# Second feed-forward: convolution with tokens on the partitions, gates shifted by DMA, only the gated units turned

## Chip, cores and metric

The kernel runs on one core of one Trainium2 chip. The metric is the device time of one execution in microseconds. A profiled execution is one execution with the hardware profiler on; its span runs from the first to the last instruction.

## What is computed

Two transformer blocks on one sequence of 256 tokens of width 2048, in float32. The first has attention, gated linear attention and a short convolution, and a feed-forward; the second has windowed attention, a state space model, and a feed-forward with a convolution. Only the last matters here:

```python
val, gate = jnp.split(h @ w_up[i], 2, axis=-1)    # h: 256 tokens x 2048, normed; val ("up") and gate: 5632 columns
gate = causal_depthwise_conv(gate, conv_w[i], conv_b[i])
x = x + (val * jax.nn.gelu(gate, approximate=False)) @ w_down[i]

def causal_depthwise_conv(x, w, b):               # along the tokens
    xp = jnp.pad(x, ((0, 0), (CONV_WIDTH_2 - 1, 0), (0, 0)))
    y = b
    for k in range(CONV_WIDTH_2):                 # CONV_WIDTH_2 = 3
        y = y + w[k] * xp[:, k:k + l]
    return y
```

## The kernel before

**Panels and pieces.** Each large product is cut into panels of 512 output columns. A panel of the feed-forward has 2048 rows of weights, 4 chunks of 512 rows; a chunk (1 MB) is one load into one of 4 slots, and is used as two pieces of 256 rows. Float32 accuracy is had by splitting both operands into a high and a low part (float32r), with three matmuls for each product: high by high, low by high, high by low. A piece is 12 matmuls of 512 columns: 2 blocks of 128 rows, 2 halves of 128 tokens, 3 matmuls. The stationary side is the activation, turned so that features lie on the partitions (xT_hi, xT_lo, hiddenT_hi, hiddenT_lo); results come out with tokens on the partitions (panels, in PSUM, two banks for each of two panels at a time).

**Who does what.** The five engines' programs are written out by hand, each in a class of its own, tied by semaphores. SyncE issues the weight loads (L370), each when the low half of the last piece of the chunk four earlier is done. ScalarE writes the high half of piece g+3 (`split`, L1225) when TensorE has finished piece g-1 (a ring of 4 pieces). VectorE writes the low half behind it (L1803). TensorE waits for `lo_split` before each piece. After each piece every engine may take one step of side work (`side.step()`): generators whose `yield`s say in which step each part is issued. On VectorE and ScalarE the step comes right behind the half of piece g+3.

**The feed-forwards.** `ffn` runs over 11 pairs of panels, gate and then up. ScalarE evacuates the gate panel into `FF1` (L1377), VectorE the up panel into `FF2`. In the first feed-forward the gate is passed through Silu, VectorE multiplies at the evacuation (L1966), and TensorE turns the product, 8 transposes of 128x128 (`tr`, L619) in one side step of the next pair's gate panel; ScalarE and VectorE write hiddenT_hi and hiddenT_lo from PSUM. In the second (`second` is true) gate and up are evacuated as they are (L1963) and both turned, 16 transposes; with features on the partitions the convolution is a multiplication by a scalar for each partition and tap, with the tokens shifted along the row: `conv2` (L2001, L2007), Gelu (L1396), the product with the turned up (`gate2`, L2019), high (L1398) and low part (L2023). The weights of the convolution lie in `V2`, one column for each block of 128 features. They are loaded in the opening as rows of 128 elements (`vectors`, L1302: seven small loads; `load_rows4`, L1283 to L1286: five more) and turned by TensorE (`turn_rows`).

**Queues.** Loads issued by ScalarE stand in its own instruction stream (shown as ACTq) and share the 16 DMA engines with SyncE's weight loads. Each adds 16 to a semaphore when it has landed.

Of the kernel before, what the change touches and what calls it, by code (L numbers as in the profile page):

```python
# [14 lines left out]
P = 128  # L15
# [75 lines left out]
class Events:  # L91
# [8 lines left out]
        mixed ffn_turned hidden_hi hidden_lo convolved gelu_ready gated_ready rows_applied  # L100
# [8 lines left out]
    LOADS = """x_load0 x_load1 x_load2 x_load3 x_load4 second_piece fourth_piece rows0 rows1 rows2 rows3 rows4 decay gla_b norm_rows dt b_proj c_proj v_bias sinks  # L109
        gate_rows0 gate_rows1 glu_rows stores""".split()  # L110
# [11 lines left out]
class Memory:  # L122
# [10 lines left out]
    def on_chip(self):  # L133
# [20 lines left out]
        self.V2 = small("vectors2", [P, 4 * KF])  # L154
# [55 lines left out]
        self.CG = sb("conv_gelu", [P, 2, S], R + 96 * K)  # L210
# [55 lines left out]
        self.ROWS = [sb(f"rows{i}", [P, P], 90 * K + R + 512 * i) for i in range(5)]  # L266
# [226 lines left out]
class Tensor:  # L493
# [8 lines left out]
    def program(self):  # L502
# [44 lines left out]
        self.ffn(plan.ffn1, side, False)  # L547
# [29 lines left out]
        self.ffn(plan.ffn2, side, True)  # L577
# [123 lines left out]
    def ffn(self, panels, side, second):  # L701
        m = self.m
        X = (m.XH, m.XL)
        for i, (gate, up) in enumerate(panels):
            if i:
                side.add(self.ffn_turn(panels[i - 1], second, spread=True))
            self.panel(gate, X, side)
            self.panel(up, X, side)
            side.finish()
        side.add(self.ffn_turn(panels[-1], second, spread=False))  # L710

    def ffn_turn(self, pair, second, spread):
# [3 lines left out]
        for kp in range(2):  # L716
            for pan in pair:
                for t in range(TT):
                    pe.wait_ge(*pan.evac[t])
            self.ffn_turns += 1  # L720
            n = self.ffn_turns
            if second:
                b0, b1 = self.bank(2 * kp), self.bank(2 * kp + 1)
                for k in range(2):
                    for t in range(TT):
                        f = (2 * kp + k) * P
                        o = slice(k * S + t * P, k * S + (t + 1) * P)
                        self.tr(b0[:, o], m.FF1[:, t, f:f + P])
                        inst = self.tr(b1[:, o], m.FF2[:, t, f:f + P])
                self.free(2 * kp, "gated_ready", n - 2 * (FF // PANEL))  # L730
                self.free(2 * kp + 1, "gated_ready", n - 2 * (FF // PANEL))
            else:
                inst = self.four(self.bank(kp), lambda k, t: m.FF2[:, t, k * P:(k + 1) * P], 2 * kp)
                self.free(kp, "hidden_lo", n)
            inst.then_inc(ev["ffn_turned"])
        for _ in range((5 if second else 4) if spread else (4 if second else 2)):
            yield
        if not spread:
            for _ in range(5 if second else 0):
                yield  # L740
# [375 lines left out]
class Scalar:  # L1116
# [161 lines left out]
    def load_rows4(self):  # L1278
        act, t, rows, ev = self.act, self.t, self.m.ROWS[4], self.ev
        vec = lambda x: x.rearrange("(k p) -> k p", p=P)  # L1280
        at = 0
        for n in ("norm2_w", "attn_norm_g_2", "ffn_norm_g_2"):
            act.dma_start(rows[at:at + KD, :], vec(t[n][0])).then_inc(ev["loaded_rows4"], 16)  # L1283
            at += KD
        act.dma_start(rows[at:at + 2, :], vec(t["gla_norm_w"][0])).then_inc(ev["loaded_rows4"], 16)
        act.dma_start(rows[at + 2:at + 26, :],  # L1286
                      t["conv_w"][0].rearrange("j (k p) -> (j k) p", p=P)).then_inc(ev["loaded_rows4"], 16)
# [6 lines left out]
    def vectors(self):  # L1294
        act, t, m, ev = self.act, self.t, self.m, self.ev
        vec = lambda x: x.rearrange("(k p) -> k p", p=P)
        cw = t["conv_w_2"][0].rearrange("j (k p) -> (j k) p", p=P)
        for i, at, n, src in ((1, 0, 88, cw[0:88, :]), (2, 0, 44, cw[88:132, :]), (2, 44, 44, vec(t["conv_b_2"][0])),
                              (3, 0, 14, vec(t["b_in_2"][0, 0:QKVU2])), (3, 14, 4, vec(t["ssm_d_2"][0])),
                              (3, 18, ST, t["ssm_a_re_2"][0].rearrange("(s q) p -> s (q p)", q=2)),  # L1300
                              (3, 34, ST, t["ssm_a_im_2"][0].rearrange("(s q) p -> s (q p)", q=2))):
            act.dma_start(m.ROWS[i][at:at + n, :], src).then_inc(ev[f"loaded_rows{i}"], 16)  # L1302
        self.load_rows4()
        for _ in range(7):
            yield
        for i, dst, n in ((1, m.V2[:, 0:88], 88), (2, m.V2[:, 88:176], 88), (3, m.V3[:, 0:50], 50),
                          (4, m.V1[:, KD:90], 74)):
# [56 lines left out]
    def ffn(self, panels, side, second, rows):  # L1364
        act, m, ev = self.act, self.m, self.ev
        n0 = 2 * len(panels) if second else 0
        for i, (gate, up) in enumerate(panels):
            if i:
                side.add(self.ffn_turn(i - 1, second, spread=True))
            self.panel(gate, side)  # L1370
            act.wait_ge(ev["multiplied"], gate.end)
            if i and second:
                act.wait_ge(ev["ffn_turned"], n0 + 2 * i)
            for t in range(TT):
                if i:
                    act.wait_ge(*panels[i - 1][1].evac[t])
                act.activation(m.FF1[:, t, :], m.ACC[:, (gate.index % 2) * TT + t, :],  # L1377
                               ACT.Copy if second else ACT.Silu, scale=m.RSTD[:, t:t + 1]).then_inc(gate.evac[t][0])
            self.panel(up, side)
            side.finish()  # L1380
        side.add(self.ffn_turn(len(panels) - 1, second, spread=False, rows=rows, pair=panels[-1]))

    def ffn_turn(self, i, second, spread, rows=None, pair=None):
# [4 lines left out]
        for kp in range(2):  # L1388
# [3 lines left out]
            if second:  # L1392
                yield
                k = n - 2 * (FF // PANEL)
                act.wait_ge(ev["convolved"], k)
                act.activation(m.CG[:, :, :], m.CG[:, :, :], ACT.Gelu).then_inc(ev["gelu_ready"])  # L1396
                act.wait_ge(ev["gated_ready"], k)
                act.activation(hh, m.CG[:, :, :], ACT.Copy).then_inc(ev["hidden_hi"])  # L1398
            else:
                act.wait_ge(ev["ffn_turned"], n)  # L1400
                act.activation(hh, m.SIDE[:, kp, :], ACT.Copy).then_inc(ev["hidden_hi"])
            yield
            if spread and kp == 0:
                yield
                if not second:
                    yield
# [287 lines left out]
class Vector:  # L1694
# [162 lines left out]
    def vectors(self):  # L1857
        for _ in range(7):
            yield
        for i in (1, 2, 3, 4):  # L1860
# [87 lines left out]
    def ffn(self, panels, side, second):  # L1948
        dve, m, ev = self.dve, self.m, self.ev
        n0 = 2 * len(panels) if second else 0  # L1950
        for i, (gate, up) in enumerate(panels):
            if i:
                side.add(self.ffn_turn(i - 1, second, spread=True))
            self.panel(gate, side)
            self.panel(up, side)
# [12 lines left out]
        side.add(self.ffn_turn(len(panels) - 1, second, spread=False))  # L1968

    def ffn_turn(self, i, second, spread):  # L1970
# [4 lines left out]
        for kp in range(2):  # L1975
            self.ffn_turns += 1
            if second:
                self.conv2(at, kp)
                yield
                self.gate2(at, kp)  # L1980
            else:
                k = slice(at + 2 * kp, at + 2 * kp + 2)
# [490 lines left out]
```

## Time and profile before

| | |
|---|---|
| median of 3 runs | 2894.95 us (2894.95 to 2894.97) |
| profiled execution | 2894.78 us, of which span 2893.5 us |
| TensorE busy | 2879.7 us, 13528 matmuls and transposes |
| VectorE, ScalarE busy | 1632.5 us, 1321.2 us |
| DMA | 536.86 MB, 186 GB/s in the mean |
| TensorE's granted clock, mean | 0.999 |

Busy times are those of one profiled execution. Matmuls overlap in the profile (each is shown longer than the distance to the next), so distances between starts say more than durations. A releaser behind an arrow is the instruction whose end let the waiting one start. PE is TensorE, ACT ScalarE, DVE VectorE, SP SyncE; ACTq and SPq are the DMA instructions on those engines' streams.

### The profile page before, as it was taken

The page shows a single profiled execution, that of the slowest core. Times are in us where ns is not written, and L with a number is a line of the kernel's source. Part 1 is how long each engine was busy: PE and PEld are TensorE (multiplying, and loading weights), DVE is VectorE, ACT ScalarE, POOL GpSimd, SP SyncE. Part 2 cuts the span into 40 slices and gives each one's busy share as a digit, 9 for nine tenths or more (in the row PEclk, how much of TensorE's full clock was granted, in tenths as well). Part 3 has the DMA queues.
Part 4 walks back from the last instruction along what each step waited for, and adds up shares of the span by engine and source line. Part 5 has one row for each costly group of instructions (what it writes and reads, how often), then busy time and mean ns, then how long its engine had stood idle before and what let it go on. Part 6 is the DMA issues. An engine that isn't in the chain of part 4 may idle for free.

```text
span 2893.5 us, 32574 instructions
## 1 busy us (share of the span) xinstructions
PE 2879.7 (100%) x13528; PEld 2379.0 (82%) x13528; DVE 1632.5 (56%) x1874; ACT 1321.2 (46%) x1627; POOL 182.2 (6%) x221
## 2 busy tenths in 40 slices
PE   9999999999999999999999999999999999999998
PEld 8878887788888888888888888887888888888887
DVE  5464555555555554554474457655755665656444
ACT  5444445444444444444454455444554444444443
POOL 0000000000000000000000029900100000000000
PEclk9999999999999999999999999999999999999999
DMA  7655454555555556555665555554655555555563
GB/s 252 197 167 194 155 192 148 174 189 189 193 188 187 189 189 190 189 190 189 205 193 183 185 175 198 171 171 153 205 188 189 188 178 189 183 193 191 187 204 131
DMA packets 279392, 536.86 MB, mean 186 GB/s; under 512 B 17361, under 2 KB 20365, under 8 KB 279245
## 3 DMA queue, kind: packets, MB, share of 16 engines
q1 hardware_dynamic: 267520, 528.52, 56.0%
q10 hardware_dynamic: 11725, 6.27, 0.8%
q8 instruction: 107, 1.75, 0.2%
q14 instruction: 40, 0.33, 0.0%
HBM read 532.65 MB, written 2.10 MB: 185 GB/s over the span
## 4 chain that ended last, share of the span: by engine, by line
PE 99%; DVE 1%; ACT 0%; issue 0%; POOL 0%; POOLq 0%; ACTq 0%; DVEq 0%
PE panels L595 32%; PE panels L597 31%; PE panels L596 31%; PE side L619 3%; DVE weights_lo L1803 0%; PE side L911 0%; PE side L608 0%; PE side L988 0%; PE side L907 0%; PE side L896 0%; PE side L775 0%; PE side L1080 0%; PE side L1081 0%; PE side L1057 0%; PE side L792 0%; PE side L809 0%
## 5 line engine op out<-in xcount | busy, mean ns | idle before, releaser
L1803 DVE TENSOR_TENSOR weights_lo<-weights,weights_hi 128x1024 fp32r<-128x1024 f32 (+1 forms) x1032 | 1252.9, 1219 | 1080.6 <-ACT weights_hi L1225 1078.0
L1225 ACT ACTIVATE weights_hi<-weights 128x1024 fp32r<-128x1024 f32 (+1 forms) x1032 | 1066.4, 1036 | 1220.2 <-PE panels L597 1205.9
L595 PE MATMUL panels<-weights_hi,xT_hi 128*128 128x512 f32 (+1 forms) x2752 | 1078.2, 392 | 0.2
L597 PE MATMUL panels<-weights_hi,xT_lo 128*128 128x512 f32 (+1 forms) x2752 | 1068.4, 388 | 0.0
L596 PE MATMUL panels<-weights_lo,xT_hi 128*128 128x512 f32 (+1 forms) x2752 | 1067.8, 388 | 0.0
L595 PEld LDWEIGHTS panels<-weights_hi,xT_hi 128*128 128x128 f32 x2752 | 516.8, 188 | 112.1 <-issue 7.3
L597 PEld LDWEIGHTS panels<-weights_hi,xT_lo 128*128 128x128 f32 x2752 | 516.6, 188 | 107.9
L596 PEld LDWEIGHTS panels<-weights_lo,xT_hi 128*128 128x128 f32 x2752 | 517.0, 188 | 103.2 <-issue 0.2
L595 PE MATMUL panels<-weights_hi,hiddenT_hi 128*128 128x512 f32 x704 | 274.9, 391 | 0.0
L597 PE MATMUL panels<-weights_hi,hiddenT_lo 128*128 128x512 f32 x704 | 274.0, 389 | 0.0
L596 PE MATMUL panels<-weights_lo,hiddenT_hi 128*128 128x512 f32 x704 | 273.9, 389 | 0.0
L597 PEld LDWEIGHTS panels<-weights_hi,hiddenT_lo 128*128 128x128 f32 x704 | 132.1, 188 | 27.4
L596 PEld LDWEIGHTS panels<-weights_lo,hiddenT_hi 128*128 128x128 f32 x704 | 132.2, 188 | 27.2
L595 PEld LDWEIGHTS panels<-weights_hi,hiddenT_hi 128*128 128x128 f32 x704 | 132.2, 188 | 27.2
L402 POOL TENSOR_TENSOR rstd<-mean_squares,minus_half 128x2 f32<-128x2 f32 x5 | 3.5, 697 | 1270.6 <-DVE mean_squares L1866 1270.6
L595 PE MATMUL panels<-weights_hi,merged2T_hi 128*128 128x512 f32 x128 | 50.4, 393 | 0.3 <-issue 0.3
L595 PE MATMUL panels<-weights_hi,mixedT_hi 128*128 128x512 f32 x128 | 50.2, 392 | 0.0
L597 PE MATMUL panels<-weights_hi,merged2T_lo 128*128 128x512 f32 x128 | 49.9, 390 | 0.0
L597 PE MATMUL panels<-weights_hi,mixedT_lo 128*128 128x512 f32 x128 | 49.9, 390 | 0.0
L596 PE MATMUL panels<-weights_lo,merged2T_hi 128*128 128x512 f32 x128 | 49.8, 389 | 0.0
L596 PE MATMUL panels<-weights_lo,mixedT_hi 128*128 128x512 f32 x128 | 49.8, 389 | 0.0
L402 POOL TENSOR_TENSOR rstd_first<-mean_squares,minus_half 128x2 f32<-128x2 f32 x1 | 0.7, 691 | 737.9 <-DVE mean_squares L1866 737.9
(354 smaller groups left out, 1912.7 us busy)
## 6 DMA issues: line engine op xcount, KB each, us to landing
weights<-in_w_in SPq DMA_DIRECT2D x162, 1024.0 KB, 5.0
weights<-in_w_up SPq DMA_DIRECT2D x88, 1024.0 KB, 5.1
weights<-in_w_ffn_gate SPq DMA_DIRECT2D x44, 1024.0 KB, 5.1
weights<-in_w_ffn_up SPq DMA_DIRECT2D x44, 1024.0 KB, 5.2
weights<-in_w_out SPq DMA_DIRECT2D x32, 1024.0 KB, 5.2
weights<-in_w_ffn_down SPq DMA_DIRECT2D x32, 1024.0 KB, 5.1
weights<-in_w_down SPq DMA_DIRECT2D x32, 1024.0 KB, 5.1
weights<-in_w_ffn_down SPq DMA_DIRECT2D x16, 768.0 KB, 4.5
```

The source lines that it names most:

```text
L402: self.pool.tensor_tensor(dst[:, 0:2], self.m.MS[:, 0:2], self.m.NHALF[:, 0:2], ALU.pow).then_inc(self.ev["rstd_ready"])
L595: pe.matmul(acc, a, wh, start=k0 + k == 0, stop=False)
L596: pe.matmul(acc, a, wl, start=False, stop=False)
L597: inst = pe.matmul(acc, b, wh, start=False, stop=k0 + k == total - 1)
L619: return self.pe.transpose(out, in_, self.m.IDENT[0:in_.shape[0], 0:in_.shape[0]])
L1225: self.act.activation(self.m.HI[:, g % PIECES, 0:n], raw, ACT.Copy).then_inc(self.ev["hi_split"])
L1803: self.dve.tensor_tensor(m.LO[:, ring, 0:n], raw, m.HI[:, ring, 0:n].bitcast(F32), ALU.subtract).then_inc(self.ev["lo_split"])
```

## The change

In the second feed-forward the convolution is done with tokens on the partitions, before anything is turned. ScalarE evacuates the gate panel into `FF1` as before and then issues, for each pair, four copies from SBUF to SBUF: the gates shifted by one token (`GS1`) and by two (`GS2`), each as one copy within partitions 0 to 127-s and one that carries the last tokens of the first half over to the first partitions of the second. The weights of the three taps and the bias are loaded from HBM for each pair as rows of 512 columns, broadcast to all 128 partitions (`WR1`, `WR2`, four loads, a panel ahead). VectorE does the convolution in six operations over both token halves at once (`conv2`), spread over the side steps of the up panel; ScalarE does one Gelu; VectorE multiplies at the evacuation of the up panel, as in the first feed-forward, and TensorE turns the product alone with the same code as there. `V2`, its three small loads and its two turns in the opening are gone. Shapes: `FF1`, `GS1`, `GS2` are [128, 2, 512] in float32.

The diff, cut to what the prediction speaks of:

```diff
+        self.GS1 = sb("gate_shifted1", [P, TT, PANEL], R + 96 * K)
+        self.GS2 = sb("gate_shifted2", [P, TT, PANEL], 80 * K + 512)
+        self.WR1 = sb("conv_rows01", [P, 2, PANEL], R + 40 * K)
+        self.WR2 = sb("conv_rows2b", [P, 2, PANEL], R + 84 * K)
...
-        for i, n, loads in ((1, 88, 1), (2, 88, 2), (3, 50, 4), (4, 74, 5)):
+        for i, n, loads in ((1, 50, 4), (2, 74, 5)):
...
-            if second:
-                b0, b1 = self.bank(2 * kp), self.bank(2 * kp + 1)
-                for k in range(2):
-                    for t in range(TT):
-                        f = (2 * kp + k) * P
-                        o = slice(k * S + t * P, k * S + (t + 1) * P)
-                        self.tr(b0[:, o], m.FF1[:, t, f:f + P])
-                        inst = self.tr(b1[:, o], m.FF2[:, t, f:f + P])
-                self.free(2 * kp, "gated_ready", n - 2 * (FF // PANEL))
-                self.free(2 * kp + 1, "gated_ready", n - 2 * (FF // PANEL))
-            else:
-                inst = self.four(self.bank(kp), lambda k, t: m.FF2[:, t, k * P:(k + 1) * P], 2 * kp)
-                self.free(kp, "hidden_lo", n)
-            inst.then_inc(ev["ffn_turned"])
-        for _ in range((5 if second else 4) if spread else (4 if second else 2)):
+            self.four(self.bank(kp), lambda k, t: m.FF2[:, t, k * P:(k + 1) * P], 2 * kp).then_inc(ev["ffn_turned"])
+            self.free(kp, "hidden_lo", n)
+        for _ in range(4 if spread else 2):
             yield
         if not spread:
-            for _ in range(5 if second else 0):
-                yield
...
+        if second:
+            side.add(self.conv_rows(panels[0][0], self.plan.out2[-1].end))
...
             self.panel(gate, side)
             act.wait_ge(ev["multiplied"], gate.end)
-            if i and second:
-                act.wait_ge(ev["ffn_turned"], n0 + 2 * i)
             for t in range(TT):
                 if i:
                     act.wait_ge(*panels[i - 1][1].evac[t])
                 act.activation(m.FF1[:, t, :], m.ACC[:, (gate.index % 2) * TT + t, :],
                                ACT.Copy if second else ACT.Silu, scale=m.RSTD[:, t:t + 1]).then_inc(gate.evac[t][0])
+            if second:
+                side.finish()
+                self.shift_gates(gate)
+                side.add(self.gelu(i, panels))
             self.panel(up, side)
...
+    def conv_rows(self, gate, end):
+        act, m, ev, t = self.act, self.m, self.ev, self.t
+        act.wait_ge(ev["multiplied"], end)
+        cols = slice(gate.col - FF, gate.col - FF + PANEL)
+        for dst, src in ((m.WR1[:, 0, :], t["conv_w_2"][0][0, cols]), (m.WR1[:, 1, :], t["conv_w_2"][0][1, cols]),
+                         (m.WR2[:, 0, :], t["conv_w_2"][0][2, cols]), (m.WR2[:, 1, :], t["conv_b_2"][0][cols])):
+            act.dma_start(dst, src.partition_broadcast(P)).then_inc(ev["loaded_conv_rows"], 16)
+        yield
+
+    def shift_gates(self, gate):
+        act, m, ev = self.act, self.m, self.ev
+        self.wait_evacuated(gate)
+        for s, dst in ((1, m.GS1), (2, m.GS2)):
+            act.dma_start(dst[s:P, :, :], m.FF1[0:P - s, :, :]).then_inc(ev["loaded_shifted"], 16)
+            act.dma_start(dst[0:s, 1, :], m.FF1[P - s:P, 0, :]).then_inc(ev["loaded_shifted"], 16)
+
+    def gelu(self, i, panels):
+        act, m, ev = self.act, self.m, self.ev
+        for _ in range(6):
+            yield
+        act.wait_ge(ev["convolved"], i + 1)
+        act.activation(m.FF1[:, :, :], m.FF1[:, :, :], ACT.Gelu).then_inc(ev["gelu_ready"])
+        if i + 1 < len(panels):
+            yield from self.conv_rows(panels[i + 1][0], panels[i][0].end)
...
         dve, m, ev = self.dve, self.m, self.ev
         n0 = 2 * len(panels) if second else 0
+        if second:
+            dve.memset(m.GS1[0:1, 0, :], 0.0)
+            dve.memset(m.GS2[0:2, 0, :], 0.0)
         for i, (gate, up) in enumerate(panels):
             if i:
-                side.add(self.ffn_turn(i - 1, second, spread=True))
+                side.add(self.ffn_turn(i - 1, spread=True))
             self.panel(gate, side)
+            if second:
+                side.finish()
+                side.add(self.conv2(i))
             self.panel(up, side)
             side.finish()
             dve.wait_ge(ev["multiplied"], up.end)
             if i:
                 dve.wait_ge(ev["ffn_turned"], n0 + 2 * i)
             for t in range(TT):
-                acc, r = m.ACC[:, (up.index % 2) * TT + t, :], m.RSTD[:, t:t + 1]
                 if second:
-                    dve.tensor_scalar(m.FF2[:, t, :], acc, r, None, ALU.mult).then_inc(up.evac[t][0])
+                    dve.wait_ge(ev["gelu_ready"], i + 1)
                 else:
                     dve.wait_ge(*gate.evac[t])
-                    dve.scalar_tensor_tensor(out=m.FF2[:, t, :], in0=acc, scalar=r, in1=m.FF1[:, t, :],
-                                             op0=ALU.mult, op1=ALU.mult).then_inc(up.evac[t][0])
...
+    def conv2(self, i):
+        dve, m, ev, step = self.dve, self.m, self.ev, self.step
+        w0, w1, w2, bias = (r[:, j, :].unsqueeze(1).to_broadcast([P, TT, PANEL]) for r in (m.WR1, m.WR2) for j in range(2))
+        g = m.FF1[:, :, :]
+        yield
+        yield
+        dve.wait_ge(ev["loaded_shifted"], 16 * 4 * (i + 1))
+        dve.wait_ge(ev["loaded_conv_rows"], 16 * 4 * (i + 1))
+        step(dve.tensor_tensor(g, g, w2, ALU.mult))
+        for shifted, w in ((m.GS1, w1), (m.GS2, w0)):
+            yield
+            step(dve.tensor_tensor(shifted[:, :, :], shifted[:, :, :], w, ALU.mult))
+            step(dve.tensor_tensor(g, g, shifted[:, :, :], ALU.add))
+        yield
+        dve.tensor_tensor(g, g, bias, ALU.add).then_inc(ev["convolved"])
+        yield
```

## Rows read from the trace of the kernel before

**Rows 1.** Page: busy times and granted clock.

```profile
PE 2879.7 (100%) x13528; PEld 2379.0 (82%) x13528; DVE 1632.5 (56%) x1874; ACT 1321.2 (46%) x1627; POOL 182.2 (6%) x221
...
PEclk9999999999999999999999999999999999999999
```

**Rows 2.** All waits of PE.

```profile
PE side L608 <- POOL identity L408: 1.6, 1, 1.6
PE side L619 <- DMA x<-in_x: 1.0, 1, 1.0
PE panels L595 <- issue: 0.3, 1, 0.3
```

**Rows 3.** Chain of work: start us, us, what, in three stretches.

```profile
48.44 0.56 PE side L619 x4
...
1036.62 0.87 PE side L619 x8
...
1081.06 0.87 PE side L619 x8
...
2239.41 1.75 PE side L619 x16
2284.70 1.75 PE side L619 x16
```

**Rows 4.** Timeline of ACT and DVE: start us, us, engine line op [idle before <-releaser].

```profile
2228.56 1.06 ACT L1225 ACTIVATE weights_hi<-weights 128x1024 fp32r<-128x1024 f32 x1 [1.60 <-PE panels L597]
...
2229.65 1.23 DVE L1803 TENSOR_TENSOR weights_lo<-weights,weights_hi 128x1024 fp32r<-128x1024 f32 x1 [1.43 <-ACT weights_hi L1225]
...
2257.53 1.27 ACT L1377 ACTIVATE ffn_gate<-panels,rstd 128x512 f32<-128x512 f32 x2 [1.54 <-PE panels L597]
```

**Rows 5.** Tile conv_gelu: duration ns min/median/max, first and last start.

```profile
L2007 DVE SCALAR_TENSOR_TENSOR conv_gelu<-side,vectors,conv_gelu x88: 470/480/485, 2196.0 to 2655.0; 128x255 f32<-128x255 f32 x44, 128x254 f32<-128x254 f32 x44
L2001 DVE TENSOR_SCALAR conv_gelu<-side,vectors x44: 533/538/545, 2195.0 to 2653.1; 128x256 f32<-128x256 f32 x44
```

**Rows 6.** Groups by form, 128x1024 operands: count, busy us, mean ns.

```profile
L2031 DVE TENSOR_TENSOR projected_a<-projected_a 128x1024 f32<-128x1024 f32 x2 | 2.4, 1220 | 0.0
...
L1683 ACT ACTIVATE merged<-merged 128x1024 f32<-128x1024 f32 x4 | 4.2, 1049 | 0.0
```

**Rows 7.** Tile ffn_hidden, evacuation in the first feed-forward.

```profile
L1966 DVE SCALAR_TENSOR_TENSOR ffn_hidden<-panels,rstd,ffn_gate x22: 741/748/751, 986.8 to 1431.8; 128x512 f32<-128x512 f32 x22
```

**Rows 8.** DMA issues: KB each, median us to landing.

```profile
weights<-in_w_up SPq DMA_DIRECT2D x88, 1024.0 KB, 5.1
...
c_twice<-in_ssm_c_re ACTq DMA_DIRECT2D x2, 128.0 KB, 2.3
```

**Rows 9.** DMA in 2454 to 2458.2, one weight load: GB/s in 40 slices, packets.

```profile
GB/s 312 234 293 410 371 429 449 351 410 449 371 390 468 371 390 410 449 371 429 410 293 234 176 117 59 0 0 0 0 0 0 0 0 0 0 0 0 0 0 0
DMA packets 459, 0.91 MB, mean 216 GB/s; under 512 B 16, under 2 KB 16, under 8 KB 459
```

**Rows 10.** DMA queue of ACT in 34 to 46: packets, MB, share.

```profile
q10 hardware_dynamic: 445, 0.15, 4.9%
```

**Rows 11.** DMA queue of SP: whole span (page), then 2885 to 2893.5 (stores).

```profile
q1 hardware_dynamic: 267520, 528.52, 56.0%
...
q1 hardware_dynamic: 848, 2.10, 64.1%
```

**Rows 12.** Timeline, DMA issues on ACT's queue: start us, us.

```profile
1441.05 4.50 ACTq L1528 DMA_DIRECT2D b_im<-in_ssm_b_im  x1
...
1762.07 0.35 ACTq L1677 DMA_DIRECT2D gate_bias_rows<-in_b_in  x1
```

**Rows 13.** Granted clock after the last matmul (third from the right), and PE's opening.

```profile
2887.50:2889.00 1.50, 0.00 (x0) 0.00 (x0) 0.67 (x2) 0.55 (x1) 0.00 (x0) 0.52 0.95 363
...
1.59 3.78 PE L608 MATMUL side<-identity 128*128 128x128 f32 x16 [1.59 <-POOL identity L408]
...
7.27 1.50 PE L608 MATMUL side<-identity 128*128 128x128 f32 x12
```

More of the change, by code:

```diff
@@ L265, in on_chip @@
         self.FF2 = sb("ffn_hidden", [P, TT, PANEL], R + 92 * K)
-        self.ROWS = [sb(f"rows{i}", [P, P], 90 * K + R + 512 * i) for i in range(5)]
+        self.ROWS = [sb(f"rows{i}", [P, P], 90 * K + R + 512 * i) for i in range(3)]
 class Plan:
@@ L546, in program @@
         self.residual(plan.out1, (m.MH, m.ML), side, rows=False, turn=True)
-        self.ffn(plan.ffn1, side, False)
+        self.ffn(plan.ffn1, side)
         side.add(self.ssm_setup())
@@ L699, in residual, with ffn @@
             side.add(self.norm_panel(p, pan, rows, turn))
-    def ffn(self, panels, side, second):
+    def ffn(self, panels, side):
         m = self.m
@@ L705, in ffn @@
             if i:
-                side.add(self.ffn_turn(panels[i - 1], second, spread=True))
+                side.add(self.ffn_turn(panels[i - 1], spread=True))
             self.panel(gate, X, side)
@@ L709, in ffn, with ffn_turn @@
             side.finish()
-        side.add(self.ffn_turn(panels[-1], second, spread=False))
-    def ffn_turn(self, pair, second, spread):
+        side.add(self.ffn_turn(panels[-1], spread=False))
+    def ffn_turn(self, pair, spread):
         pe, ev, m = self.pe, self.ev, self.m
@@ L1378, in ffn, with ffn_turn @@
                                ACT.Copy if second else ACT.Silu, scale=m.RSTD[:, t:t + 1]).then_inc(gate.evac[t][0])
+            if second:
+                side.finish()
+                self.shift_gates(gate)
+                side.add(self.gelu(i, panels))
             self.panel(up, side)
             side.finish()
-        side.add(self.ffn_turn(len(panels) - 1, second, spread=False, rows=rows, pair=panels[-1]))
-    def ffn_turn(self, i, second, spread, rows=None, pair=None):
+        side.add(self.ffn_turn(len(panels) - 1, spread=False, rows=rows, pair=panels[-1]))
+    def conv_rows(self, gate, end):
[20 more added lines that the diff above has]
+            yield from self.conv_rows(panels[i + 1][0], panels[i][0].end)
+    def ffn_turn(self, i, spread, rows=None, pair=None):
         act, m, ev = self.act, self.m, self.ev
@@ L1391, in ffn_turn @@
             hh = m.HH[:, at + 2 * kp:at + 2 * kp + 2, :]
[L1392 to L1401, printed above, removed]
+            act.wait_ge(ev["ffn_turned"], n)
+            act.activation(hh, m.SIDE[:, kp, :], ACT.Copy).then_inc(ev["hidden_hi"])
             yield
@@ L1859, in vectors @@
             yield
-        for i in (1, 2, 3, 4):
+        for i in (1, 2):
             self.dve.wait_ge(self.ev["vectors"], i + 1)
@@ L1950, in ffn @@
         n0 = 2 * len(panels) if second else 0
+        if second:
+            dve.memset(m.GS1[0:1, 0, :], 0.0)
+            dve.memset(m.GS2[0:2, 0, :], 0.0)
         for i, (gate, up) in enumerate(panels):
             if i:
-                side.add(self.ffn_turn(i - 1, second, spread=True))
+                side.add(self.ffn_turn(i - 1, spread=True))
             self.panel(gate, side)
+            if second:
+                side.finish()
+                side.add(self.conv2(i))
             self.panel(up, side)
@@ L1976, in ffn_turn @@
             self.ffn_turns += 1
[L1977 to L1982, printed above, removed]
-                self.dve.wait_ge(self.ev["hidden_hi"], self.ffn_turns)
-                self.dve.tensor_tensor(m.HL[:, k, :], m.SIDE[:, kp, :], m.HH[:, k, :].bitcast(F32),
-                                       ALU.subtract).then_inc(self.ev["hidden_lo"])
+            k = slice(at + 2 * kp, at + 2 * kp + 2)
+            self.dve.wait_ge(self.ev["hidden_hi"], self.ffn_turns)
+            self.dve.tensor_tensor(m.HL[:, k, :], m.SIDE[:, kp, :], m.HH[:, k, :].bitcast(F32),
+                                   ALU.subtract).then_inc(self.ev["hidden_lo"])
             yield
```

79 lines of the change are left out of this document (21 added, 58 removed).

## Prediction

> **What bounds the kernel now.** First the page's busy times: TensorE is busy for all but 13.8 us of the span, VectorE for 56% and ScalarE for 46%, at a granted clock of 9 tenths or more in every slice [rows 1]. Then the waits of TensorE: three, 2.9 us together, all in the opening [rows 2]. So only two kinds of edit move the end: fewer or shorter TensorE instructions, and anything that makes TensorE wait where it does not wait today. The stage to read is the second feed-forward. The chain view shows the first feed-forward too, whose turning already has the form that the change gives the second: a turn there is 8 transposes in 0.87 us and pairs of panels follow at 1081.06 - 1036.62 = 44.44 us; in the second it is 16 transposes in 1.75 us and the step is 2284.70 - 2239.41 = 45.29 us [rows 3]. Taking the turn out, 43.57 us are left for the 16 pieces of a pair, 2.72 us each. That is the pulse to which all else is compared.
>
> **TensorE's own work.** 88 of 176 transposes of the stage go (gate and up were both turned, now the product alone): 0.88 us by the blocks, 0.85 by the steps, I take 0.87; 11 pairs give 9.6 us. Two of four turns of weight rows go from the opening, half of 0.56 us [rows 3], 0.3. These are on the path in full, since TensorE waits for nothing there. Sum: 9.9 us. The profiled execution (2894.78 us, a span of 2893.5 and 1.3 around it) stands 0.17 under the median of 2894.95, from which I count: 2885.1 if nothing else changed.
>
> **The reserve under which the rest must stay.** ScalarE's high half of piece g+3 starts when TensorE starts piece g (it waits for TensorE each time) and takes 1.06 us; VectorE's low half follows and takes 1.23, so a low half is ready some 2.6 us after the start of piece g and due at 3 x 2.72 = 8.2: a reserve of 5.6 us [rows 4]. VectorE's removed work of a pair is two sets of 2 x 0.54 and 4 x 0.48 us, 6.0 in all, and two products [rows 5]. Its new work is six tensor_tensor over 128x1024 at 1.22 [rows 6], 7.3 us plus some 0.1 for each settled step; the combined multiplication takes the place of the present evacuation, and costs 0.75 each in the first feed-forward [rows 7]. In the middle two side steps 1.23 + 2.44 stand against a pulse of 2.72, a lag of 2 us in a reserve of 5.6: nothing. ScalarE does one Gelu over 1024 elements (1.05 by its activations of that size [rows 6]) instead of two over 512. The gate panel of a pair becomes, step for step, that of the first feed-forward, where TensorE does not wait. The last turn before the down projection also takes the first one's form, which had no wait. The four row broadcasts are issued a panel ahead. None of this moves the end.
>
> **The shift.** New, and without a row in the trace, are four copies from SBUF to SBUF for each pair, issued on ScalarE's queue behind the gate's evacuation; VectorE waits for all four in the third side step of the up panel, behind which its low halves are queued, and behind those TensorE. Call the start of the up panel U. The wait stands behind the low half of piece 5; piece 6 is due at U + 16.3, and needs before it the first multiplication and its low half, 1.3 + 1.2. The copies must therefore have landed by U + 13.8. If 520 KB were spread over 16 engines as the weights are, that would be easy: 1 MB lands in 5 us [rows 8].
>
> How many engines does a copy use? One weight load is 512 packets of 2 KB, and its window holds 16 packets under 512 B beside them, one completion for each of 16 engines [rows 9]. In the window with the twelve small loads of vectors, ScalarE's queue shows 445 packets [rows 10]. The twelve bring 150 KB in rows of 512 B, 300 packets; so 145 are completions, where 12 x 16 = 192 would be all engines. Their row counts are 88, 44, 44, 14, 4, five times 16, 2 and 24. The largest divisor up to 16 of each is 11, 11, 11, 14, 4, five times 16, 2 and 12, and these add up to 145 exactly. I read that a copy goes to as many engines as the largest divisor up to 16 of its count of partitions. The shift by one copies partitions 0 to 126: 127 is prime, so one engine. The shift by two has 126 rows and gets 14 engines. The Trainium skill says the same of a shape that no row here has: its page "DMA: Bandwidth & Descriptors", section "Why a DMA increments its semaphore by 16 and not by 1", has 127 partitions put everything on one engine, and the lowest-numbered one.
>
> Price: 127 rows of 4096 B are 520 KB. The stores at the end read SBUF too: 2.10 MB in 64.1% of 16 engines over 8.5 us is 24.1 GB/s for one engine. Over the whole span the loads show 528.52 MB in 56.0%, 20.4 GB/s; the best slices of the weight window show 468 / 16 = 29 GB/s, its usual ones about 410 / 16 = 26 [rows 9, 11]. I take the stores' 24.1: 21.6 us. (The skill's page gives about 27 GiB/s for an engine, section "Specifications"; by it 17.9 us and an end some 41 us earlier than mine. The trace's mean rates are lower, and decide.) Beside it the same engine carries its sixteenth of each weight load, 65.5 KB or 2.7 us; two loads are issued between U and the wait, 5.4 us; and 9 rows of the other shift, 1.5 us. The evacuation ends at U + 1.5 (1.27 us long [rows 4]) and its own wait makes it 1.6. From issue to landing 128 KB take 2.3 us [rows 8], nearly all fixed. Landing: 1.6 + 2.3 + 21.6 + 5.4 + 1.5 = U + 32.4. One thing can alter the order: in the one place where a copy put 128 packets on each engine (b_re), the next issue held ScalarE for 4.50 us [rows 12]. If the shift holds it too, high halves stop earlier, TensorE waits first at piece 3, and fewer weights compete: U + 30 to 32. I take U + 32.0.
>
> VectorE resumes: 0.1 + 1.27 + 1.23 puts the low half of piece 6 at U + 34.6, a wait of 34.6 - 16.3 = 18.3 us. Then it is behind with all the rest, at t from there: low half 7 at 3.85, 8 at 7.7, bias at 8.95, low half 9 at 10.2; ScalarE's Gelu to 10.1, four issues of 0.35 [rows 12] to 11.5, high half 10 to 12.6; low half 10 at 14.1; two evacuations of 0.75 to 15.6, for which the turn waits. On schedule that turn would be at 4 x 2.72 = 10.9: 4.7 us more. After the gap the clock will be down: with TensorE idle at the end it is 0.52 between 2887.5 and 2889, the half level (1.2 GHz), and in the opening 16 small matmuls took 3.78 us, while from 7.27 on 12 took 1.50 [rows 13]. Pieces 6 and 7 at the half level cost up to 2.7 us each, but the turn waits until 15.6 anyway, so I count nothing.
>
> Sum: 11 x (18.3 + 4.7) = 253.0, less 1.4 for the last pair, which issues no rows: 251.6. 2894.95 - 9.9 + 251.6 = 3136.7, say **3137 us**.
>
> **Bounds.** Low: 29.2 GB/s (17.8 us), a fixed part of 1.7, no weights beside it, 1.2 for the other shift: landing at U + 22.3, wait 8.6, 11 x 13.3 - 1.4 = 145 us, 3030. High: 20.4 GB/s (25.5 us), 2.5 fixed, three loads at 3.2, 1.8: U + 41.0, wait 27.3, 11 x 32.0 - 1.4 = 351 us, 3236. The range is 3030 to 3235.
>
> **Rivals.** (a) The copy is spread over several engines, by a regrouping of its shape before it is issued. Four engines are enough: 5.4 us of data land before U + 13.8 even behind the two weight loads. Then only the 9.9 us remain: 2885.1, faster. For it: every large load in the trace uses all 16, and no row shows an odd count. Against: 88 and 44 rows went to 11 engines, not to 16, although their 512 B rows could have been regrouped. (b) Spread, but a tensor_tensor with a row repeated over both token halves runs at half pace (no such row of this size exists; 1.22 is from plain operands). Four of six at 2.44 put the low half of piece 9 at U + 25.3 and the evacuation at U + 30.8, against a turn due at U + 27.2: 3.6 x 11 = 40 us, 2925. It decides only when VectorE's extra passes 5 us a pair; nothing in the trace speaks for it. (c) One engine, but VectorE's wait does not show because TensorE has reserve: excluded, since that engine needs 8 x 2.7 for weights, 23.1 for shifts and 2.7 for rows, 47.4 us in a pair of 44.4; even perfectly overlapped it would lose 3 us a pair.
>
> **Chances.** One engine, 3137: 0.86. Spread, 2885: 0.11. Spread with slow operands, 2925: 0.02. Something that cancels: 0.01. A measurement of this kernel can tell about 0.2% from no change. Faster 0.11, same 0.01, slower 0.88. The range of 3030 to 3235 leaves out the spread cases and a little of the first, 2 in 10 at most.
>
> **What the profile after would show.** Right: shifts landing some 25 to 31 us after issue where the 126 rows would need 3; VectorE's first multiplication idle before it for 20 us on a DMA, 11 times; TensorE waiting for weights_lo 11 times, by 15 to 20 us; a low clock in the slices from three quarters on; a step of pairs near 66.5 us; turns of 0.87 us. Wrong: landings near 3 to 6 us and a step of 44.4. If the landing is as said but ScalarE's queue is held, the wait splits between pieces 3 and 6 with the same sum. The prediction falls if the count of engines does not follow the divisor.

## The result and the profile after

The changed kernel takes 3124.09 us (median of 4 runs, 3123.31 to 3125.24) against 2894.95 before (2894.13 to 2894.97): ratio 1.0793, 95% interval 1.078 to 1.0807, 7.9% slower. The profiled execution has a span of 3122.0 us and a mean granted clock of 0.969. The forecast was 3137.

The page after: busy times, granted clock in 40 slices, ScalarE's DMA queue (packets, MB, share) and the chain of work by engine and by line.

```profile
PE 2926.3 (94%) x13438; PEld 2402.2 (77%) x13438; DVE 1634.1 (52%) x1788; ACT 1313.6 (42%) x1614; POOL 183.1 (6%) x221
...
PEclk9999999999999999999999999999888898888999
...
q10 hardware_dynamic: 21196, 29.18, 3.1%
...
PE 82%; DMA 7%; DVE 4%; ACTq 4%; ACT 1%; issue 1%; SPq 0%; POOL 0%
```

TensorE has 90 matmuls fewer than in [rows 1], and yet shows 46.6 us more busy time and 6% of the span idle: the matmuls behind each gap run at the lower clock, and the clock's line first shows an 8 in the slice from 2185 us on, where the second feed-forward's pairs run. The chain, which was TensorE alone, now passes through a DMA and ScalarE's queue.

The waits after (in total, times, longest; PE had three small ones in [rows 2]):

```profile
ACT ffn_gate L1392 <- DVE ffn_gate L2010: 176.0, 11, 17.0
PE panels L597 <- DVE weights_lo L1807: 170.6, 23, 9.6
...
DVE ffn_gate L2004 <- DMA gate_shifted<-ffn_gate: 161.9, 11, 15.4
ACT weights_hi L1213 <- issue: 136.0, 21, 11.6
```

VectorE waits 11 times, once a pair, for the shifted gates, and TensorE twice a pair for VectorE's low halves. One pair, in order (timeline of ACT, DVE and PE: start us, us, what, in brackets the idle time before and what ended it):

```profile
2364.82 1.27 ACT L1361 ACTIVATE ffn_gate<-panels,rstd 128x512 f32<-128x512 f32 x2 [1.60 <-PE panels L599]
2366.17 0.64 ACTq L1384 DMA_DIRECT2D gate_shifted<-ffn_gate  x1
2366.84 8.13 ACTq L1385 DMA_DIRECT2D gate_shifted<-ffn_gate  x1
2375.01 0.84 ACTq L1384 DMA_DIRECT2D gate_shifted<-ffn_gate  x1
2375.88 1.77 ACTq L1385 DMA_DIRECT2D gate_shifted<-ffn_gate  x1
2377.69 3.90 ACT L1213 ACTIVATE weights_hi<-weights 128x1024 fp32r<-128x1024 f32 x4 [11.61 <-issue]
...
2396.41 1.23 DVE L2004 TENSOR_TENSOR ffn_gate<-ffn_gate,conv_rows2b 128x1024 f32<-128x1024 f32 x1 [14.14 <-DMA gate_shifted<-ffn_gate]
2397.68 1.22 DVE L1807 TENSOR_TENSOR weights_lo<-weights,weights_hi 128x1024 fp32r<-128x1024 f32 x1
...
2407.38 1.06 ACT L1392 ACTIVATE ffn_gate<-ffn_gate 128x1024 f32<-128x1024 f32 x1 [16.15 <-DVE ffn_gate L2010]
2407.38 0.82 ACTq L1377 DMA_DIRECT2D conv_rows<-in_conv_w  x2
...
2411.51 1.41 DVE L1975 SCALAR_TENSOR_TENSOR ffn_hidden<-panels,rstd,ffn_gate 128x512 f32<-128x512 f32 x2
...
2380.06 0.79 PE L597 MATMUL panels<-weights_hi,xT_hi 128*128 128x512 f32 x1 [7.12 <-DVE weights_lo L1807]
2398.95 0.80 PE L597 MATMUL panels<-weights_hi,xT_hi 128*128 128x512 f32 x1 [8.82 <-DVE weights_lo L1807]
2413.18 1.06 PE L621 MATMUL side<-identity,ffn_hidden 128*128 128x128 f32 x8 [0.67 <-DVE ffn_hidden L1975]
```

The up panel starts at U = 2364.6. The first copy, partitions 0 to 126, is issued at once; the next issue, a copy of a single row, then holds ScalarE for 8.13 us. High halves stop, so TensorE waits a first time, at the fourth piece (number 3), until 2380.06. The copies have landed at 2396.4 = U + 31.8, the low half of piece 6 is ready at U + 34.3, and TensorE's second wait ends there. The bracket of 8.82 us is less than piece 6 was late, because the pieces before it ran partly at half pace: with a pulse of 2.72 from 2380.06 it was due at 2388.2 and came 10.7 late, as piece 3, due at 2372.8, came 7.3 late.

Over the time from the issue to the landing, the DMA view (GB/s in 40 slices of 2366 to 2397, then the issues with KB and time to landing):

```profile
GB/s 56 5 11 5 26 26 26 26 26 26 26 26 29 148 222 233 82 48 26 87 219 381 386 378 370 365 362 159 48 37 29 24 24 26 26 24 26 29 21 26
...
weights<-in_w_up SPq DMA_DIRECT2D x2, 1024.0 KB, 14.3
gate_shifted<-ffn_gate ACTq DMA_DIRECT2D x1, 508.0 KB
gate_shifted<-ffn_gate ACTq DMA_DIRECT2D x1, 504.0 KB
```

Eight slices at 26 in a row, and again at the end at 21 to 29: that is what one engine moves, where 16 show some 410 [rows 9]. The hump at 148 to 233 is the 504 KB of the shift by two, spread, that at 360 to 386 two loads of weights, which land after 14.3 us where the median was 5.1 [rows 8]. That fits a sixteenth of each queued on the slow engine; with the copy spread, in e1_spread below, the median of these loads is 5.2.

### The profile page after: what moved, and what is told of

The parts are those of the page before. It is cut to its first block, busy times and chain, and to the rows that moved or that the text cites. A ratio compares the mean times of both kernels' runs of the same rounds, so it can differ in the third digit from the quotient of the medians.

```text
span 3122.0 us, 32387 instructions
## 1 busy us (share of the span) xinstructions
PE 2926.3 (94%) x13438; PEld 2402.2 (77%) x13438; DVE 1634.1 (52%) x1788; ACT 1313.6 (42%) x1614; POOL 183.1 (6%) x221
## 4 chain that ended last, share of the span: by engine, by line
PE 82%; DMA 7%; DVE 4%; ACTq 4%; ACT 1%; issue 1%; SPq 0%; POOL 0%
PE panels L597 26%; PE panels L599 26%; PE panels L598 26%; DMA gate_shifted<-ffn_gate 7%; ACTq L1385 3%; PE side L621 2%; DVE weights_lo L1807 2%; DVE ffn_gate L2008 1%; DVE gate_shifted L2007 1%; ACTq L1384 1%; DVE ffn_hidden L1975 0%; ACT ffn_gate L1361 0%; DVE ffn_gate L2004 0%; ACT weights_hi L1213 0%; ACTq L1377 0%
## 5 line engine op out<-in xcount | busy, mean ns | idle before, releaser
L597 PE MATMUL panels<-weights_hi,xT_hi 128*128 128x512 f32 (+1 forms) x2752 | 1103.3, 401 | 170.8 <-DVE weights_lo L1807 170.6
L598 PE MATMUL panels<-weights_lo,xT_hi 128*128 128x512 f32 (+1 forms) x2752 | 1087.1, 395 | 0.0
L599 PE MATMUL panels<-weights_hi,xT_lo 128*128 128x512 f32 (+1 forms) x2752 | 1086.2, 395 | 0.0
L597 PEld LDWEIGHTS panels<-weights_hi,xT_hi 128*128 128x128 f32 x2752 | 529.7, 192 | 296.1 <-DVE weights_lo L1807 182.1
L599 PEld LDWEIGHTS panels<-weights_hi,xT_lo 128*128 128x128 f32 x2752 | 528.2, 192 | 111.9
L598 PEld LDWEIGHTS panels<-weights_lo,xT_hi 128*128 128x128 f32 x2752 | 530.0, 193 | 106.4 <-issue 0.2
L2004 DVE TENSOR_TENSOR ffn_gate<-ffn_gate,conv_rows2b 128x1024 f32<-128x1024 f32 x11 | 13.5, 1225 | 161.9 <-DMA gate_shifted<-ffn_gate 161.9
L1392 ACT ACTIVATE ffn_gate<-ffn_gate 128x1024 f32<-128x1024 f32 x11 | 11.7, 1062 | 176.0 <-DVE ffn_gate L2010 176.0
```

The lines of the kernel that those rows point to most:

```text
L597: pe.matmul(acc, a, wh, start=k0 + k == 0, stop=False)
L598: pe.matmul(acc, a, wl, start=False, stop=False)
L599: inst = pe.matmul(acc, b, wh, start=False, stop=k0 + k == total - 1)
L1392: act.activation(m.FF1[:, :, :], m.FF1[:, :, :], ACT.Gelu).then_inc(ev["gelu_ready"])
L2004: step(dve.tensor_tensor(g, g, w2, ALU.mult))
```

## The experiments

The theory: all the loss comes from the 127-partition copy going to one DMA engine. Rivals: that ScalarE's held queue is the cause, that the slower clock behind the gaps is part of the bill, or that the copies or VectorE's added work cost by their amount. Unless a diff says otherwise, only the copies of `shift_gates` differ from the changed kernel. The kernel before stood beside every group of runs at 2894.49 to 2894.94 us.

**e1_spread and e10_126: cut the copy so that it spreads.**

```diff
-            act.dma_start(dst[s:P, :, :], m.FF1[0:P - s, :, :]).then_inc(ev["loaded_shifted"], 16)
+            for a, b in ((0, 112), (112, P - s)) if s == 1 else ((0, P - s),):
+                act.dma_start(dst[a + s:b + s, :, :], m.FF1[a:b, :, :]).then_inc(ev["loaded_shifted"], 16)
-        dve.wait_ge(ev["loaded_shifted"], 16 * 4 * (i + 1))
+        dve.wait_ge(ev["loaded_shifted"], 16 * 5 * (i + 1))
```

e10_126 has 126 in place of 112, so 126 partitions and 1.

> The long copy of the shift by one is cut into 112 and 15 partitions, everything else is the changed kernel. One engine (my theory: a copy goes to the largest divisor up to 16 of its partitions, and 127 has none): the cut copy uses 16 engines, lands with the others within about 6 us of its issue, far before the start of the up panel + 13.8 us, TensorE waits for nothing in the stage, a pair takes 44.4 us and the kernel 2885.1 us, 9.9 below the kernel before; a little more (up to 5 us in all) if five issues on ScalarE, some 0.65 us each, delay the high half of piece 3, whose reserve they nearly use up. Rival 1 (copies from SBUF to SBUF are slow whatever the count): no better than 3124. Rival 2 (the loss is VectorE's or ScalarE's new work, or the row broadcasts): 3124 too, since none of that changes.

> The shift-by-one copy is cut into 126 partitions (14 x 9, fourteen engines) and 1. Theory (the largest divisor not above 16 sets the engines; the last partition alone is one packet): as with 112 and 15, 2886.5 us, 2885 to 2889. Rival (it is the size of the copy that was slow, one partition less changes nothing): 3124 us.

Measured: 2886.53 us (0.9972 of the kernel before, 0.9961 to 0.9983) and 2888.39 us (0.9977, 0.9968 to 0.9987). The same bytes, one or fifteen partitions less in the first copy, and 236 to 238 us are gone. The turns of e1_spread in its chain of work, start us and us:

```profile
2371.74 0.87 PE side L621 x8
2416.18 0.87 PE side L621 x8
```

A step of 44.44 us, to the hundredth that of the first feed-forward [rows 3]. No wait of VectorE on a DMA is left, nor one of TensorE on a low half. Both versions are faster than the kernel before, by 0.2 to 0.3%, and so faster than the changed one by far.

**e6_none: no copies at all.** GS1 and GS2 are set to 0 once and never written by a copy, and the wait for them is gone; the output leaves out the convolution's taps on the two earlier tokens.

```diff
-        for s, dst in ((1, m.GS1), (2, m.GS2)):
-            act.dma_start(dst[s:P, :, :], m.FF1[0:P - s, :, :]).then_inc(ev["loaded_shifted"], 16)
-            act.dma_start(dst[0:s, 1, :], m.FF1[P - s:P, 0, :]).then_inc(ev["loaded_shifted"], 16)
...
-        dve.wait_ge(ev["loaded_shifted"], 16 * 4 * (i + 1))
```

> The shifted gates are zeros, set once before the stage: no copy is issued and VectorE does not wait for one; all other work of the change stays. This leaves out the taps of the two earlier tokens. My theory: 2885 us, and within 2 us of the kernel with the cut copy, so that the copies cost nothing once they are spread. Rival 2 (new work on VectorE or ScalarE, or the row broadcasts): stays near 3124, or clearly above 2885.

Measured: 2884.79 us (0.9966, 0.9954 to 0.9979). VectorE's and ScalarE's new work is all in this kernel and costs nothing that shows; the copies, spread, cost 1.7 us in all. Of that, 1.1 us is a single wait of TensorE in e1_spread, for VectorE's product before the last turn (`PE side L621 <- DVE ffn_hidden L1976: 1.1, 1, 1.1`), which e6_none does not show. The whole stage loses 3124.09 - 2884.79 = 239.3 us to the copies of the changed kernel, 21.75 a pair.

**e2_four, e3_two, e9_seven: how many engines are enough.** The same edit as e1_spread with the cut at 124 (4 x 31), 122 (2 x 61) and 119 (7 x 17).

> The shift by one is cut into 124 and 3 partitions. By the divisor, 124 = 4 x 31 goes to 4 engines: 31 rows of 4 KB on each, some 5 us at the 0.16 us a row that one engine showed. Landing 12 to 15 us after the start of the up panel, where 13.8 is the deadline: between 2885 and 2900 us, likeliest 2887. If engines were given by ceil(rows / 8) or by any rule that is not the divisor, it would equal the kernel with 112 and 15.

> The shift by one is cut into 122 and 5 partitions. By the divisor, 122 = 2 x 61 goes to 2 engines: 61 rows on each, 9.7 us where one engine needed 20.2 for 127. Landing near 20 us after the start of the up panel instead of 31.8, so TensorE is some 6 us late at piece 6 and a further 2 to 4 us behind in what follows: 11 x 9 above 2885, 2960 to 3000, likeliest 2980. By any rule that is not the divisor it equals the kernel with 112 and 15.

> The shift-by-one copy is cut into 119 partitions (119 = 7 x 17, so seven engines, 17 partitions with 34 packets of 4096 B each... one packet of 4096 B per partition, hence 17 per engine) and 8. At 0.159 us a packet an engine has 2.7 us of work, against 4.9 us on four engines. Theory (what costs at four engines is the held issue of the five copies and the late landing, both shrinking with packets per engine): the fourth piece is no longer late and the landing comes before U+13.8; 2887 to 2895 us, likeliest 2889. Rival (only a spread over nearly all engines frees the queue): about 2915 us.

| cut | engines by the divisor | longest share of the main copy, partitions | time, us | ratio to before |
|---|---|---|---|---|
| 127 (changed kernel) | 1 | 127 | 3124.09 | 1.0793 |
| 122 + 5 | 2 | 61 | 3010.54 | 1.0401 (1.0386 to 1.0415) |
| 124 + 3 | 4 | 31 | 2949.66 | 1.019 (1.0174 to 1.0206) |
| 119 + 8 | 7 | 17 | 2898.22 | 1.0012 (1.0002 to 1.0021) |
| 126 + 1 | 14 | 9 | 2888.39 | 0.9977 |
| 112 + 15 | 16 | 7 | 2886.53 | 0.9972 |

The order is that of the divisor and not that of the size: 126 and 127 partitions lie 236 us apart, 122 and 124 between them. The DMA view shows the engines themselves where little else moves. In e3_two, from 2389 to 2411 in 40 slices:

```profile
GB/s 395 142 0 15 30 45 22 48 53 127 201 231 238 134 108 160 212 380 395 343 235 287 268 287 279 290 290 268 179 48 52 49 48 49 56 52 48 52 48 48
```

The last eleven slices, behind the weights, stand at 48 to 56 GB/s, twice the rate of one engine.

But each of the three runs came out slower than expected, e2_four by 63 us. Its timelines of ACT, DVE and PE in one pair (U = 2366.3):

```profile
2367.83 1.43 ACTq L1385 DMA_DIRECT2D gate_shifted<-ffn_gate  x2
2369.29 2.07 ACTq L1386 DMA_DIRECT2D gate_shifted<-ffn_gate  x1
2371.39 1.67 ACTq L1385 DMA_DIRECT2D gate_shifted<-ffn_gate  x1
2373.09 0.64 ACTq L1386 DMA_DIRECT2D gate_shifted<-ffn_gate  x1
2373.77 3.90 ACT L1213 ACTIVATE weights_hi<-weights 128x1024 fp32r<-128x1024 f32 x4 [6.03 <-issue]
...
2383.06 1.22 DVE L2005 TENSOR_TENSOR ffn_gate<-ffn_gate,conv_rows2b 128x1024 f32<-128x1024 f32 x1 [4.70 <-DMA gate_shifted<-ffn_gate]
...
2376.14 0.50 PE L597 MATMUL panels<-weights_hi,xT_hi 128*128 128x512 f32 x1 [1.54 <-DVE weights_lo L1808]
...
2385.60 0.50 PE L597 MATMUL panels<-weights_hi,xT_hi 128*128 128x512 f32 x1 [1.00 <-DVE weights_lo L1808]
```

Two things were late. The five issues take ScalarE to U + 7.4, where those of e1_spread take 4.0 us in all (4.01 idle before its next high half): 1.54 us of TensorE at piece 3. And the landing is at U + 16.7, 2.9 after the deadline of U + 13.8: TensorE waits 1.00 us at piece 6, then 0.63 and 0.64 at two later ones and 1.13 at the turn. These waits are 4.9 us, in a pair that takes 50.8 us for the 44.4 of e6_none; in the mean e2_four loses 5.9 us a pair, and its waits for low halves and products, 47.3 us in all, are most of its 64.9. The rest was not traced. In e9_seven nothing waits for a copy any more, and TensorE's 11 waits for low halves, 8.2 us in all, stand at piece 3 behind an issue time of 5.25 us; they are 8.2 of the 13.4 us that it lies above e6_none. e3_two landed at U + 21.8, where I had expected some 20, and its waits for low halves are 7.6 us a pair for the expected 6. So my expectation of e2_four failed in two steps: the landing was put at U + 12 to 15, and the issues, which have a price on the path too, at nothing; in e9_seven it is the issues alone that are seen.

**e4_double: a second slow copy.** The shift by two is cut into 113 partitions (a prime) and 13.

```diff
-            act.dma_start(dst[s:P, :, :], m.FF1[0:P - s, :, :]).then_inc(ev["loaded_shifted"], 16)
+            for a, b in (((0, 127),), ((0, 113), (113, 126)))[s - 1]:
+                act.dma_start(dst[a + s:b + s, :, :], m.FF1[a:b, :, :]).then_inc(ev["loaded_shifted"], 16)
```

> The shift by two, 126 partitions on 14 engines in the changed kernel, is cut into 113 and 13. 113 is prime: by the divisor it goes to one engine too, the same one, behind the shift by one. 113 rows more at 0.159 us, less the 9 rows it carried before: 16.5 us later in each pair. 3124 + 11 x 16.5 = 3305 us (3280 to 3330). If the one engine were chosen anew for each copy, the two would run side by side and the time stay near 3124, at most 10 above.

Measured: 3293.36 us, 1.1377 (1.136 to 1.1394), 15.4 us a pair more than the changed kernel, in the range and 12 us under its middle. 126 partitions were fast; 113 of them in one copy are not. In its chain the queue is held twice, and the DMA view from 2411 to 2460 shows which engine the second slow copy got:

```profile
2413.14 8.48 ACTq L1386
2421.65 0.64 ACTq L1385
2422.32 16.25 ACTq L1385
2438.60 19.49 DMA gate_shifted<-ffn_gate
...
GB/s 398 30 10 17 23 27 23 27 27 28 27 27 27 27 27 23 27 27 27 27 27 27 27 64 28 27 102 358 383 371 369 145 42 25 25 25 25 27 25 8
```

Apart from the weights the rate stays at 23 to 28 GB/s after both copies are issued, where two engines would show some 52: both slow copies went to the same one.

**e5_last: the slow copy issued last**, so that no copy stands behind it in the queue.

```diff
-            act.dma_start(dst[s:P, :, :], m.FF1[0:P - s, :, :]).then_inc(ev["loaded_shifted"], 16)
             act.dma_start(dst[0:s, 1, :], m.FF1[P - s:P, 0, :]).then_inc(ev["loaded_shifted"], 16)
+        for s, dst in ((2, m.GS2), (1, m.GS1)):
+            act.dma_start(dst[s:P, :, :], m.FF1[0:P - s, :, :]).then_inc(ev["loaded_shifted"], 16)
```

> The same four copies, the one of 127 partitions issued last. In the changed kernel the issue behind it holds ScalarE for some 8 us, so TensorE is late first at piece 3 (by 7.3 us) and again at piece 6. With the long one last ScalarE is free after 3 to 4 us, piece 3 is on time, and all of the wait stands at piece 6. My theory, that the landing on the one engine sets the end: it is issued some 1.5 us later and lands 1 to 2 us later, 3124 + 0 to 20 us, likeliest 3137. Rival (the held queue is what costs): 11 x 7 us less, near 3045.

Measured: 3152.63 us, 1.089 (1.0874 to 1.0907), 28.5 us more than the changed kernel and above my range; the rival, a faster kernel, falls. Waits, and TensorE's timeline in one pair (evacuation at 2372.86, so U = 2372.7):

```profile
PE panels L597 <- DVE weights_lo L1808: 225.2, 11, 20.9
...
ACT weights_hi L1213 <- issue: 51.2, 24, 3.9
...
2409.60 0.79 PE L597 MATMUL panels<-weights_hi,xT_hi 128*128 128x512 f32 x1 [20.46 <-DVE weights_lo L1808]
```

ScalarE is no longer held (3.9 us at most, against 11.6), the wait at piece 3 is gone, and the one at piece 6 has taken it over whole. VectorE resumes at 2407.07 = U + 34.4, 2.6 later than in the changed kernel, since the long copy is issued 2.1 us later; 11 x 2.6 = 28.6. The held queue is a consequence and not the cause: without it the same landing costs as much.

**e7_warm and e8_fill: keep the clock up.** Small matmuls on the identity, into a bank that nobody reads, before pieces 3 and 6 of each up panel.

```diff
             ring = g % PIECES
+            if pan in [up for _, up in self.plan.ffn2] and g - pan.first in (3, 6):
+                self.warm(28 if g - pan.first == 3 else 40)
             pe.wait_ge(self.ev["lo_split"], g + 1)
```

e7_warm has 50 and 80 there.

> The changed kernel with small matmuls into an unused bank, before TensorE's waits for pieces 3 (50 of them) and 6 (80) of each up panel, as filling for the gaps of 7 and 9 us, so that the granted clock does not fall. My step in the prediction: the half clock behind the gap costs nothing, because the turn waits for VectorE and ScalarE longer than that: granted clock 0.99 or more in the stage, and the time within 6 us of 3124. Rival (the clock costs what its slow matmuls show, some 1.7 us twice in a pair): 11 x 2 to 3.4 us less, 3087 to 3102.

> The one-engine copy stays; TensorE gets 28 small matmuls before the fourth piece and 40 before the seventh piece of each up panel, 56 and 80 instructions in the trace at 0.11 us, so 6.2 us of work in a gap of 7.3 and 8.9 us in one of 9.6 to 10.7. The filling ends before the low half that the piece waits for, so nothing is delayed and the granted clock should stay at 1.00 through the gaps. Theory (the half clock behind a gap costs nothing, because the low halves then come from VectorE one every 3.65 us and the turn waits for VectorE's product): 3124 us, 3119 to 3129. Rival (the 3.5 us at half pace behind the second gap are on the path): about 1.7 us less for each of the 11 pairs, 3105 us.

e7_warm took 3204.7 us, 1.1071 (1.1053 to 1.109). It missed because each of these matmuls is two instructions in the trace, so the filling was longer than the gaps and was itself what TensorE was late by (chain of work):

```profile
2395.55 11.16 PE side L612 x100
2414.89 17.86 PE side L612 x160
```

It says nothing of the clock. e8_fill, with the size read from these two rows, does: 3127.49 us (3124.86 to 3128.8), 1.0802 (1.0786 to 1.0818), the same as the changed kernel within 0.2%. In the windows view of the changed kernel and then of e8_fill (window, length, busy of PE, PEld, DVE, ACT, POOL, then granted clock, DMA share, GB/s):

```profile
2390.00:2400.00 10.00, 1.18 (x4) 0.86 (x4) 3.55 (x3) 1.06 (x1) 0.00 (x0) 0.69 0.05 18
2400.00:2405.00 5.00, 5.00 (x15) 4.00 (x14) 4.86 (x6) 0.00 (x0) 0.00 (x0) 0.60 0.25 56
```

```profile
2390.00:2400.00 10.00, 10.00 (x84) 9.73 (x83) 0.25 (x1) 1.20 (x2) 0.00 (x0) 1.00 0.11 41
2400.00:2410.00 10.00, 7.11 (x32) 5.15 (x31) 9.83 (x9) 0.00 (x0) 0.00 (x0) 1.00 0.30 98
```

In the changed kernel the clock falls in the gap and the first products behind it run at half pace, with TensorE busy in the whole window. With the gap filled the clock is 1.00 in both windows, and TensorE is instead idle for 2.9 of the 10 us behind it (7.11 busy) while VectorE is busy for 9.83: the low halves and the convolution's passes come no faster. What the clock took, the engine would have waited.

## Why the prediction was right

**The TensorE saving** of 9.9 us: e6_none is 9.9 under the kernel before that ran beside it (2894.69). A turn in e1_spread takes 0.87, as taken.

**One engine.** Right: eight slices at 26 GB/s, twice that on two engines, and six versions of the copy in the order of the divisor. By the Trainium skill ("DMA: Bandwidth & Descriptors", "Why a DMA increments its semaphore by 16 and not by 1"), 127 partitions put all on one engine; the trace agrees. Which engine it is was not read.

**The landing**: U + 31.8 for 32.0, but by errors that cancel; that the two agree within 0.2 us is luck. The engine moved 26 GB/s, not the stores' 24.1 [rows 11], so 520 KB took 20.0 us, not 21.6. With 1.5 for the issue and the counted 5.4 and 1.5 for weights and the other shift, 3.4 us are left for the fixed part, not 2.3; how much of that belongs to the weights the runs don't separate. The Trainium skill's figure of about 27 GiB/s for an engine ("DMA: Bandwidth & Descriptors", "Specifications") gives an estimate of 17.9 us for the data; the measured rate lies between it and mine, nearer to mine.

**ScalarE's held queue**: named as possible, with the wait split between pieces 3 and 6 and the same sum. So it came: 7.3 and 10.7 us behind the schedule of the pulse, 18.0 for the forecast 18.3, and e5_last puts all of it at piece 6. The signs that I gave (TensorE waiting 11 times by 15 to 20 us, VectorE idle for 20 us on the DMA) were those of a queue that is not held: the changed kernel shows 23 waits of at most 9.6 us and 14.7 us of VectorE in the mean, e5_last 11 waits of TensorE at 20.5 us in the mean and 11 of VectorE at 25.4.

**The way to the turn** is the term that was mis-sized: 4.7 us a pair, of which 3.4 came (the turn starts at U + 48.6, due at U + 27.2, less 18.0). The four row broadcasts were put in series behind the Gelu, 1.4 us; in the timeline they start with it at 2407.38, and the high half follows at 2409.28, 1.1 us earlier than by my sum. The turn starts 1.3 us earlier than by it; with 0.3 at the wait the sum is 1.6 us too high in this pair. Over the ten steps from one gate's evacuation to the next, the changed kernel takes 65.98 us in the mean and e6_none 44.43: a loss of 21.55 for the 23.0 of the sum, 14.5 us too much. In the last pair the sum was too low: from its evacuation to the end the changed kernel takes 23.3 us more than e6_none, where 23.0 less 1.4 for the rows had been put. TensorE waits 2.69 us for VectorE's product there, against 0.67 in the pair shown, and 1.11 in e1_spread, where no copy is waited for: this turn has less reserve than the others. That leaves 14.5 - 1.7 = 12.8 us for the 12.3 by which 251.6 is above the measured 239.3. The step named in the prediction, 66.5 us, does not follow from its own sum, which gives 44.4 + 23.0 = 67.4; measured in the pair shown: 2430.63 - 2364.82 = 65.8.

**The clock** was counted at nothing; e8_fill bears that out.

**Rivals.** (a) a spread copy at 2885.1 did not happen, but was priced well: e1_spread is 2886.5. The sentence in it that four engines are enough was wrong (e2_four is 64.6 us above 2885.1), and the prediction's own terms would have shown it: 1.6 + 2.3 + 5.4 + 5.4 for the weights + 1.5 for the other shift put the landing at U + 16.2, behind the deadline of 13.8; it came at U + 16.7. The five issues on ScalarE were left out too. (b) operands repeated over both token halves run at full pace, 1225 ns in the page's row of L2004 against 1220 for plain ones [rows 6]; its 40 us fall. (c) stays excluded.

## What to carry to other kernels

Before a DMA is issued, look at the count of partitions it moves: if its largest divisor up to 16 is small, cut it where the count divides well, 127 into 112 and 15 or 126 and 1, and not by size. Do the sum for the whole chain behind the transfer (issue, shared engine, landing, the first instruction that waits, what is queued behind that), against the reserve of the engine that sets the pace; in this kernel a landing after U + 13.8 cost, and one before it did not. A slow clock behind a gap was no cost of its own here, since another engine set the pace behind it (3127.5 us with the gaps filled, 3124.1 without).

## What was not expected of the hardware

- The issue behind the one-engine copy holds the issuing engine for 7.8 to 8.7 us, and behind a second such copy for 16.25 us (e4_double); in [rows 12] it was 4.50 behind 128 packets on each engine. What sets it is open. It is not the packets on one engine alone: in the cut versions, where the copy of the remaining partitions stands between, the row copy's issue took 1.91 us with 119 partitions on seven engines, 2.07 with 124 on four and 0.96 with 122 on two.
- An issue from SBUF to SBUF takes 0.64 to 0.84 us where nothing holds it, against 0.41 to 0.45 for the row broadcasts in the same trace: four or five of them in a row are 3 to 4 us of ScalarE, about as much as four high halves.
